# Opening loads and first mean rearranged, and one reciprocal of the end made by GpSimd as a power

## The reference

```python
def rmsnorm(x, g):
    y = x * lax.rsqrt(jnp.mean(x * x, axis=-1, keepdims=True) + EPS)
    return y * g

def swiglu(x, w_gate, w_up, w_down):
    return (jax.nn.silu(x @ w_gate) * (x @ w_up)) @ w_down

def layer_forward(x, p_i, norm_g, w1g, w1u, w1d, w2g, w2u, w2d, w_pe, w_pg, mix):
    x = x + 0.5 * swiglu(rmsnorm(x, norm_g[0]), w1g, w1u, w1d)
    x = x + mix(rmsnorm(x, norm_g[1]))       # attention, then a recurrent block
    x = x + 0.5 * swiglu(rmsnorm(x, norm_g[2]), w2g, w2u, w2d)
    x = x + (p_i @ w_pe) * jax.nn.sigmoid(rmsnorm(x, norm_g[3]) @ w_pg)
    return x
# two layers, then the final norm:
y = rmsnorm(x, final_norm_g)
```

## Time and profile before

| | us |
|---|---|
| median of three runs | 1190.08 (1189.02 to 1190.3) |
| the profiled execution | 1188.74 |
| its span | 1187.0 |
| TensorE busy | 1171.9 (99%) |
| VectorE busy | 793.3 (67%) |
| ScalarE busy | 583.4 (49%) |
| GpSimd busy | 155.5 (13%) |
| mean granted TensorE clock, share of full speed | 0.997 |
| TensorE's longest wait, before the last mean | 1.9 |

### The profile page before, as it was taken

One profiled execution on the slowest core, in us unless ns is written; L12 is line 12 of the kernel. 1 busy time (PEld: TensorE's weight loads), 2 busy tenths in 40 slices (PEclk: granted clock), 3 DMA queues, 4 the chain that ended last, 5 costly groups with the idle time before them and its releaser, 6 DMA issues.

```text
span 1187.0 us, 23338 instructions
## 1 busy us (share of the span) xinstructions
PE 1171.9 (99%) x8992; PEld 1163.4 (98%) x8992; DVE 793.3 (67%) x1175; ACT 583.4 (49%) x862; POOL 155.5 (13%) x190
## 2 busy tenths in 40 slices
PE   9999999999999999999999999999999999999996
PEld 9999999999999999999999999999998999999996
DVE  7665655677768666565886655556989856655566
ACT  6444444466645444434564443434795544443353
POOL 0000011212232000012220000111307300000122
PEclk9999999999999999999999999999999999999998
DMA  6555444743345454354464454445453654444542
GB/s 240 180 175 166 141 160 150 272 141 107 107 156 189 162 177 161 130 168 167 155 212 149 170 177 140 150 160 189 150 166 124 202 180 151 172 155 143 173 146 97
DMA packets 37645, 193.22 MB, mean 163 GB/s; under 512 B 4017, under 2 KB 6209, under 8 KB 26065
## 3 DMA queue, kind: packets, MB, share of 16 engines
q1 hardware_dynamic: 35968, 186.81, 46.9%
q0 software_dynamic: 1040, 4.51, 1.0%
q10 hardware_dynamic: 576, 1.05, 0.3%
HBM read 188.78 MB, written 3.58 MB: 162 GB/s over the span
## 4 chain that ended last, share of the span: by engine, by line
PE 93%; DVE 4%; ACT 2%; DMA 1%; issue 1%; SPq 0%; DVEq 0%; ACTq 0%
PE bank L1189 30%; PE bank L1190 30%; PE bank L1191 30%; PE bank L1222 1%; DVE w_lo L797 1%; DMA raw<-in_up 1%; DVE conv L931 1%; DVE u_ext L944 0%; ACT w_hi L518 0%; PE bank L1236 0%; PE bank L1206 0%; PE bank L1238 0%; DVE conv L960 0%; PE bank L1250 0%; PE bank L1263 0%
## 5 line engine op out<-in xcount | busy, mean ns | idle before, releaser
L518 ACT ACTIVATE w_hi<-raw 128x1024 fp32r<-128x1024 f32 (+2 forms) x410 | 370.7, 927 | 341.4 <-PE bank L1191 328.2
L797 DVE TENSOR_TENSOR w_lo<-raw,w_hi 128x1024 fp32r<-128x1024 f32 (+2 forms) x410 | 449.4, 1114 | 79.2 <-ACT w_hi L518 77.2
L1189 PE MATMUL bank<-xg_hi,w_hi 128*128 128x288 f32 x1536 | 456.6, 297 | 0.6 <-DVE w_lo L828 0.4
L1190 PE MATMUL bank<-xg_lo,w_hi 128*128 128x288 f32 x1536 | 453.3, 295 | 0.0
L1191 PE MATMUL bank<-xg_hi,w_lo 128*128 128x288 f32 x1536 | 451.1, 294 | 0.0
L1189 PEld LDWEIGHTS bank<-xg_hi,w_hi 128*128 128x128 f32 x1536 | 288.8, 188 | 1.7 <-issue 1.1
L1191 PEld LDWEIGHTS bank<-xg_hi,w_lo 128*128 128x128 f32 x1536 | 289.1, 188 | 0.0
L1190 PEld LDWEIGHTS bank<-xg_lo,w_hi 128*128 128x128 f32 x1536 | 288.3, 188 | 0.4
L1189 PE MATMUL bank<-h_hi,w_hi 128*128 128x288 f32 x704 | 208.0, 295 | 0.0
L1190 PE MATMUL bank<-h_lo,w_hi 128*128 128x288 f32 x704 | 207.7, 295 | 0.0
L1191 PE MATMUL bank<-h_hi,w_lo 128*128 128x288 f32 x704 | 206.6, 294 | 0.0
(11 more groups left out here) (188 smaller groups left out, 1272.4 us busy)
## 6 DMA issues: line engine op xcount, KB each, us to landing
raw<-in_up SPq DMA_DIRECT2D x85, 1024.0 KB, 4.8
raw<-in_down SPq DMA_DIRECT2D x64, 704.0 KB, 4.0
raw<-in_qkv SPq DMA_DIRECT2D x24, 512.0 KB, 4.6
raw<-in_ple SPq DMA_DIRECT2D x16, 640.0 KB, 3.8
raw<-in_lru_in SPq DMA_DIRECT2D x12, 512.0 KB, 4.7
raw<-in_lru_o SPq DMA_DIRECT2D x8, 640.0 KB, 3.8
raw<-in_wo SPq DMA_DIRECT2D x4, 1024.0 KB, 5.2
raw<-in_lru_g SPq DMA_DIRECT2D x8, 512.0 KB, 5.2
```

What stands on the lines that cost most here:

```text
L518: nc.scalar.activation(w_hi[slot][:, cols], raw[slot][:, cols], ACT.Copy).then_inc(w_hi_done, 1)
L797: nc.vector.tensor_tensor(w_lo[slot][:, cols], raw[slot][:, cols], w_hi[slot][:, cols].bitcast(F32), ALU.subtract).then_inc(w_lo_done, 1)
L1189: nc.tensor.matmul(out, w_hi[slot][:, cols], hi[:, k, 0:width], start=start, stop=False)
L1190: nc.tensor.matmul(out, w_hi[slot][:, cols], lo[:, k, 0:width], start=False, stop=False)
```

## The change

Four edits. (1) The load of `vecs` is cut in two: the 8 columns of the first gains go first and have their own semaphore, the other 154 columns go behind x and ahead of group 1's weights. ScalarE and VectorE wait for the first at the start, and for the second behind group 2's weight parts. (2) ScalarE splits both parts of group 1's weights before it squares x, and VectorE both parts before it adds the squares. (3) The first mean is done before tile 14 of group 1 and not before tile 6. (4) The second token half's last `rstd` is made by GpSimd: it fills `square` with -1 after its last sum, waits for the second root, and raises `std` to that power (144 columns); VectorE waits for this and has one reciprocal less.

```diff
--- before.py
+++ after.py
@@ -123,7 +123,7 @@
 
 
 
-WARM_UP, MEAN_AT = 18, 6
+WARM_UP, MEAN_AT = 18, 14
 TOKEN_HALVES = (slice(0, TOK // 2), slice(TOK // 2, TOK))
 
 LAST_PIECES = ((0, 0, 4), (0, 4, 8), (1, 0, 4), (1, 4, 6), (1, 6, 8))
@@ -272,7 +272,7 @@
         raw_first = [sem(f"raw_first{piece}") for piece in range(3)]
         first_hi_done, first_lo_done = sem("first_hi_done"), sem("first_lo_done")
         x_landed = [sem(f"x_landed{piece}") for piece in range(4)]
-        vecs_landed, p_landed = sem("vecs_landed"), sem("p_landed")
+        first_gain_landed, vecs_landed, p_landed = sem("first_gain_landed"), sem("vecs_landed"), sem("p_landed")
         past_landed, state_landed = sem("past_landed"), sem("state_landed")
         kv_stored, tails_stored = sem("kv_stored"), sem("tails_stored")
         y_stored = sem("y_stored")
@@ -282,6 +282,7 @@
         x_new, xg_hi_done, xg_done = sem("x_new"), sem("xg_hi_done"), sem("xg_done")
         squared, summed_squares, first_squared = sem("squared"), sem("summed_squares"), sem("first_squared")
         last_squared, first_added = sem("last_squared"), sem("first_added")
+        second_rstd_done = sem("second_rstd_done")
         consts, mean_done, std_done, rstd_done = sem("consts"), sem("mean_done"), sem("std_done"), sem("rstd_done")
         gate_in_done, gate_act_done = sem("gate_in_done"), sem("gate_act_done")
         hidden_done, hidden_hi_done, hidden_lo_done = sem("hidden_done"), sem("hidden_hi_done"), sem("hidden_lo_done")
@@ -341,10 +342,11 @@
         @block.sync
         def _(sp):
 
-            sp.dma_start(vecs[:], a["vecs"]).then_inc(vecs_landed, 16)
+            sp.dma_start(vecs[:, 0:KD], a["vecs"][:, 0:KD]).then_inc(first_gain_landed, 16)
             first = PHASES[0]
             for piece, (ks, (lo, hi)) in enumerate(FIRST_PIECES):
                 sp.dma_start(x[:, ks[0]:ks[-1] + 1, :], a["x"][:, ks[0]:ks[-1] + 1, :]).then_inc(x_landed[piece], 16)
+            sp.dma_start(vecs[:, KD:], a["vecs"][:, KD:]).then_inc(vecs_landed, 16)
 
             for phase in PHASES:
                 def load(turn, n, b, phase=phase):
@@ -487,6 +489,13 @@
             pool.dma_start(a["tails"], tails[:]).then_inc(tails_stored, 16)
             for stage in range(6, 9):
                 squares(stage)
+
+            pool.wait_ge(summed_squares, STAGES * KD - 1)
+            nc.gpsimd.memset(square[:], -1.0).then_inc(squared, 1)
+            pool.wait_ge(squared, SQUARES_BEFORE[-1] + KD - 1)
+            pool.wait_ge(std_done, STAGES + 1)
+            nc.gpsimd.tensor_tensor(rstd[:, TOKEN_HALVES[1]], std[:, TOKEN_HALVES[1]], square[:, TOKEN_HALVES[1]],
+                                    ALU.pow).then_inc(second_rstd_done, 1)
             pool.wait_ge(kv_stored, 32)
             pool.wait_ge(tails_stored, 16)
 
@@ -537,7 +546,7 @@
                 act.dma_start(raw[0][:, lo * P:hi * P], group_dram(PHASES[0], 0)[0, :, lo * P:hi * P]) \
                     .then_inc((*raw_first, raw_landed[0])[piece], 16)
             nc.scalar.preload_act_table_set("sqrt_and_others")
-            act.wait_ge(vecs_landed, 16)
+            act.wait_ge(first_gain_landed, 16)
             for piece, (ks, (lo, hi)) in enumerate(FIRST_PIECES):
                 act.wait_ge(x_landed[piece], 16)
                 for k in ks:
@@ -545,12 +554,13 @@
                 act.wait_ge((*raw_first, raw_landed[0])[piece], 16)
                 nc.scalar.activation(w_hi[0][:, lo * P:hi * P], raw[0][:, lo * P:hi * P], ACT.Copy) \
                     .then_inc(w_hi_done if piece % 2 else first_hi_done, 1)
-            w_split((PHASES[0], None, 1, 1), 0)
+            for part in range(2):
+                w_split((PHASES[0], None, 1, 1), part)
             for ks in (slice(0, KD // 2), slice(KD // 2, KD)):
                 nc.scalar.activation(first_squares[:, ks, :], x[:, ks, :], ACT.Square).then_inc(first_squared, 1)
-            w_split((PHASES[0], None, 1, 1), 1)
             for part in range(2):
                 w_split((PHASES[0], None, 2, 2), part)
+            act.wait_ge(vecs_landed, 16)
             act.wait_ge(consts, 2)
 
             def log_stay(pair):
@@ -820,7 +830,7 @@
                 nc.vector.scalar_tensor_tensor(out=x[:, k, :], in0=product, scalar=factor, in1=x[:, k, :],
                                                op0=ALU.mult, op1=ALU.add).then_inc(x_new, 1)
 
-            dve.wait_ge(vecs_landed, 16)
+            dve.wait_ge(first_gain_landed, 16)
             for piece, (ks, (lo, hi)) in enumerate(FIRST_PIECES):
                 for k in ks:
                     xg_low(0, k)
@@ -828,7 +838,8 @@
                 nc.vector.tensor_tensor(w_lo[0][:, lo * P:hi * P], raw[0][:, lo * P:hi * P],
                                         w_hi[0][:, lo * P:hi * P].bitcast(F32), ALU.subtract) \
                     .then_inc(w_lo_done if piece % 2 else first_lo_done, 1)
-            w_split((PHASES[0], None, 1, 1), 0)
+            for which in range(2):
+                w_split((PHASES[0], None, 1, 1), which)
             dve.wait_ge(first_squared, 2)
             for step, width in enumerate((KD // 2, KD // 4)):
                 dve.wait_ge(first_added, step)
@@ -837,9 +848,9 @@
             dve.wait_ge(first_added, 2)
             nc.vector.tensor_tensor(sum_squares[:], first_squares[:, 0, :], first_squares[:, 1, :], ALU.add) \
                 .then_inc(summed_squares, KD)
-            w_split((PHASES[0], None, 1, 1), 1)
             for which in range(2):
                 w_split((PHASES[0], None, 2, 2), which)
+            dve.wait_ge(vecs_landed, 16)
 
             def qkv_out(n, o):
 
@@ -1169,10 +1180,12 @@
             dve.wait_ge(x_gained, KD)
             for half, lo, hi in LAST_PIECES:
                 cols = TOKEN_HALVES[half]
-                if lo == 0:
-                    dve.wait_ge(std_done, STAGES + half)
+                if half == 0 and lo == 0:
+                    dve.wait_ge(std_done, STAGES)
                     nc.vector.reciprocal(rstd[:, cols], std[:, cols]).then_inc(rstd_done, 1)
-                    dve.wait_ge(rstd_done, STAGES + half)
+                    dve.wait_ge(rstd_done, STAGES)
+                if half == 1 and lo == 0:
+                    dve.wait_ge(second_rstd_done, 1)
                 scale = rstd[:, cols].unsqueeze(1).broadcast_to([P, hi - lo, TOK // 2])
                 nc.vector.tensor_tensor(y_rows[:, lo:hi, cols], y_rows[:, lo:hi, cols], scale, ALU.mult) \
                     .then_inc(out_ready, 1)
```

## The result

The changed kernel takes 1209.63 us (median of 5 runs, 1209.32 to 1211.87) against 1189.62 for the kernel before in the same comparison: ratio 1.0167, 95% interval 1.0156 to 1.0178. It is 20 us slower. The forecast was 1189.85, in a range up to 1193.8.

The account below looks back on a forecast made before the run. TensorE, busy 1171.9 of 1187.0 us, bounds the kernel; only its waits, the opening and the end could be gained. Opening -1.10 plus end +0.87 gave -0.23 us, from 1190.08 to 1189.85, range 1188.3 to 1193.8.

Parts of the forecast that it names:

- The term that failed: At the end, GpSimd's power of 144 columns was taken to last 2.3 us, scaled from VectorE's reciprocal.
- The estimate of 2.1 us: At the end, the power at about twice VectorE's time, by the skill's engine selection; the end would cost +0.67 us.
- The end of the range: Upper limit set for GpSimd's power at the end: 30 plain columns, 41 ns a column, 6.3 us.
- the sum: Whole kernel: -1.10 us at the start and +0.87 us at the end give -0.23 us.
- Rival (b): At the end, a long power, 6.3 us, gives +3.77 us in all, 1193.85; decides from 4.9 us; chance 0.24.
- the standstill: At the end, VectorE's two-input products wait until GpSimd's power is through, 1.42 us late.
- The mean: In the opening, moving the first mean from tile 6 to tile 14 removes TensorE's wait, worth 0.90 us.
- The cover at group 3: In the opening, slack before TensorE needs group 3's weights is almost exactly used up; loss 0 to 0.3 us, taken 0.
- The loads: In the opening, 77 KB moved behind x lets x land earlier: 0.20 us gained, between 0 and 0.4.
- Opening together: All changes at the kernel's start: -1.10 us, between -0.6 and -1.3.
- The empty wire: Between the last stores the wire is empty for 0.55 us, so dropping VectorE's reciprocal saves 0.55 and not 0.99 us.
- The median: Starting time for the whole kernel: 1190.08 us over the runs, 1.34 above the profiled execution; same difference applied.

Follow-up runs that it names:

- the opening alone: The changed kernel with VectorE's second reciprocal back and no power: 1189.45 us against 1190.18 for the kernel before, ratio 0.9992.
- the mean alone: The kernel before with both splits of group 1 ahead of the squares and the first mean at tile 14: 1189.32 us against 1190.32.
- the better end: The changed kernel with VectorE's second reciprocal back and the second half stored as 2, 3, 3 chunks: 1189.16 us against 1190.32 for before.
- the sixteen columns: The kernel before with GpSimd's power for the last 16 columns only, VectorE's reciprocal for the other 128: 1190.86 us against 1190.18.
- the power alone: The kernel before with GpSimd's power of 144 columns in place of VectorE's second reciprocal: 1211.38 us against 1190.18, ratio 1.0178.
- the loads alone: The kernel before with the vectors' load cut in two and nothing else: 1190.21 us against 1190.32, ratio 1.0.
- the plain work: The kernel before with four unused GpSimd additions of 288 columns after the second root: 1191.43 us against 1190.18.
- the powers beside the stream: The kernel before with unused GpSimd powers, then 16 additions, beside the first phase's steady groups: 1189.69 us against 1190.32.

## Why the prediction was wrong

**The term that failed** is "a power is at least two such steps, a logarithm and an exponential: 0.41 + 2 x 0.95 = 2.3 us". The power took 23.39 us, ten times as much. The fixed part was right (0.38 against 0.41); the column costs 160 ns, 117 of GpSimd's plain columns of 1.37 ns, where 6.6 x 2 were taken. VectorE's reciprocal, from which that came, did not carry over to another operation on another engine. (Its ratio of 4.8 also set a slope against an average that holds the fixed part; by VectorE's slope, (1.22 - 0.82) / 384 = 1.04 ns, it is 6.0 and the power 2.8 us, which would have changed little.) The estimate of 2.1 us beside it is as far off. The end of the range, "30 plain columns, 41 ns, 6.3 us", was no bound from a row either, and the text itself said that nothing bounds the power from above. With the term of the sum put at its measured size the method gives the result: the power would end at 1179.14 + 23.39 = 1202.53, and the third product, which began at 1181.45 + 0.99, would come 20.1 us later; measured 20.24. Rival (b) had the right sign and the right cause, a power that is too long, at a quarter of the size. Its threshold of 4.9 us rested on the standstill: without it such a power ends at 1184.04 and costs 1.6 us, so that with the forecast opening the kernel would be only 0.5 us slower and not 2.4.

**The standstill** was wrong for the power. The prediction had charged 1.42 us for it; the first two products took 1.43 us beside the power, as without it. The earlier trace rows show the standstill for additions, and the additions in the power's place did disturb the same products (2.02 against 1.43 us). What held for additions was carried over to an instruction of another kind. The rule that the prediction took from the Trainium skill, "SBUF — State Buffer", "Who interferes with whom" (the second one waits for the whole of the first's instruction), agrees with the additions and not with the power: 14 weight parts of two inputs ran at their full speed beside 40 us of powers. The measurement decides. It would fit all of these rows if an instruction that spends its time in arithmetic held the read port for little of it; that is an argument, and no run shows the port itself.

**The mean** was right: 0.91 us of wait gone at TensorE (0.90 forecast). The cover at group 3 was used up, and 0.2 us of the 0 to 0.3 were lost, where the sum took 0. The reason is the reciprocal behind the mean: it began at 21.42, 0.44 us later than before where 0.1 to 0.3 were forecast. The sum left out two hand-overs of 0.1 us, from the mean to the root (20.71 to 20.82) and from the root to the reciprocal (21.32 to 21.42).

**The loads** show nothing of the 0.20 us. The first activation came 0.02 and 0.04 us earlier in two traces, and from execution to execution it moves by over half a microsecond. The term took it that x lands earlier by the wire time of the bytes moved from ahead of it; no run shows that, and what x waits for was not found. The price was not hidden at ScalarE, which waited 0.51 us for group 1's weights and not 0.30; it cost TensorE nothing, because the mean stood at tile 14.

**Opening together:** 0.71 us in the traces at 366 us, and 0.73 by the medians of the opening alone (not clear of the noise), against a forecast of 1.10 with a range from 0.6.

**The empty wire** of 0.55 us was read rightly: shrinking the third piece took 0.33 us from it.

**The median.** The prediction started from 1190.08; in the comparison the kernel before took 1189.62, so the -0.23 us of the sum stand against +20.01. The profiled execution of before, on which the sum rests, was also a lucky one in the opening: its first product began at 8.10 us, and in the nine other executions profiled between 8.05 and 9.41.

## What to carry to other kernels

Before work is moved to an engine that has no row for that operation, measure the operation by itself, at two sizes: here one run would have told that a GpSimd power costs 0.38 us and 0.160 us a column, 23.4 us for a half that VectorE does in 1.05, and that no more than 12 columns fit into the 2.3 us that were free. An estimate by analogy to another engine's operation is no bound; if the sign hangs on it, the range has to say so. A load moved ahead of another delays something: look at who waits for what now comes later. Where the last stores are back to back, look for the moment at which the wire is empty, and make the piece behind it smaller.

## What the runs showed of the hardware

- GpSimd's float32 power of two tensors takes 0.38 us and 0.160 us for each column of 128 partitions (144 and 16 columns measured, exponent -1; with 1.5 and 0.5 at most 9% more at 32 columns). It runs beside VectorE's instructions with two SBUF inputs without delaying them: 14 weight parts at 1.22 or 1.23 us. GpSimd's additions (0.79 us for 288 columns) delay them, to 1.51 to 1.69 us, and are delayed.
- TensorE's granted clock fell to 1.2 GHz for about 3.4 us near 900 us, behind TensorE's waits for y_lo, in the profiled executions of the changed kernel, the opening alone, the mean alone, the better end and the sixteen columns, and not in those of before, the power alone, the loads alone, the plain work and the powers beside the stream, all with the same 1.9 us of waits. In the changed kernel 0.76 us of lead went there. It fell in all four executions with the mean at tile 14 and in one of the six with the mean at tile 6; the mean granted clock over the timed executions does not differ (0.9963 in the opening alone and in its before). Whether the shift of the opening makes the fall likelier stays open.
- Another 0.16 us of the changed kernel's lead went between 573 and 609 us. It was not looked into.
